# Level products on quarters of the array's columns, with a weight rounding and a bank eviction moved earlier in each head

## The reference

```
o_inter = einsum('bhtk,bhkv->bhtv', qb * exp(cum), state)
rel     = cum[t] - cum[s]                      # cum = cumsum(log_f)
decay   = exp(where(tri, rel, -inf))
scores  = einsum('bhtk,bhsk,bhtsk->bhts', qb, kb, decay)
o       = o_inter + einsum('bhts,bhsv->bhtv', scores, vb)
state   = state * exp(last) + einsum('bhsk,bhsv->bhkv', kb * exp(last - cum), vb)
```

## Time and profile before

| | |
|---|---|
| median of three runs | 2038.23 us |
| the profiled execution, its own time | 2038.05 us |
| its span in the trace | 2036.3 us |
| PE busy | 2027.9 us, 100% (rounded) of the span |
| DVE, ACT, POOL busy | 974.2, 785.8, 855.4 us |
| granted clock of TensorE | 1.0 of full speed |

### The profile page before, as it was taken

One profiled execution on the slowest core, in us unless ns is written; L12 is line 12 of the kernel. 1 busy time (PEld: TensorE's weight loads), 2 busy tenths in 40 slices (PEclk: granted clock), 3 DMA queues, 4 the chain that ended last, 5 costly groups with the idle time before them and its releaser, 6 DMA issues.

```text
span 2036.3 us, 24472 instructions
## 1 busy us (share of the span) xinstructions
PE 2027.9 (100%) x9822; PEld 1659.3 (81%) x9822; DVE 974.2 (48%) x1486; ACT 785.8 (39%) x1128; POOL 855.4 (42%) x357
## 2 busy tenths in 40 slices
PE   9999999999999999999999999999999999999999
PEld 7888888888888888888888888888877788888887
DVE  4588878634321313434463242454366646324242
ACT  6455656534222224522432222246266643222222
POOL 4334333544444444444444444453422234444444
PEclk9999999999999999999999999999999999999999
DMA  5222222342323232222323223232311122322323
GB/s 178 83 83 74 75 92 73 125 146 86 108 94 97 93 102 95 94 96 90 104 94 104 93 93 104 93 114 93 94 62 55 56 77 93 104 93 95 103 93 114
DMA packets 55265, 194.31 MB, mean 95 GB/s; under 512 B 6128, under 2 KB 6640, under 8 KB 55152
## 3 DMA queue, kind: packets, MB, share of 16 engines
q1 hardware_dynamic: 55152, 192.75, 29.4%
HBM read 190.62 MB, written 2.10 MB: 95 GB/s over the span
## 4 chain that ended last, share of the span: by engine, by line
PE 97%; DVE 1%; ACT 0%; DMA 0%; SPq 0%; issue 0%; DVEq 0%
PE ps L1356 30%; PE ps L1358 29%; PE ps L1357 29%; PE ps L1682 1%; PE ps L1715 1%; PE ps L1706 1%; PE ps L1644 1%; PE ps L1643 1%; PE ps L1642 1%; PE ps L1492 1%; PE ps L1364 0%; PE ps L1394 0%; PE ps L1514 0%; DMA w_raw<-in_panels 0%; PE ps L1516 0%; PE ps L1501 0%
## 5 line engine op out<-in xcount | busy, mean ns | idle before, releaser
L352 POOL TENSOR_TENSOR w_lo<-w_raw,w_hi 128x1024 fp32r<-128x1024 f32 x353 | 855.2, 2426 | 1169.0 <-ACT w_hi L371 1149.6
L1356 PE MATMUL ps<-a_hi,w_hi 128*128 128x512 f32 x1472 | 581.0, 395 | 2.2 <-DVE arena L783 1.9
L1358 PE MATMUL ps<-a_hi,w_lo 128*128 128x512 f32 x1472 | 573.5, 390 | 0.0
L1357 PE MATMUL ps<-a_lo,w_hi 128*128 128x512 f32 x1472 | 573.3, 389 | 0.0
L371 ACT CAST w_hi<-w_raw 128x1024 fp32r<-128x1024 f32 x353 | 366.2, 1042 | 323.7 <-PE ps L1358 290.9
L1356 PE MATMUL ps<-b_hi,w_hi 128*128 128x512 f32 x1176 | 458.5, 390 | 0.3 <-DVE x L817 0.2
L1358 PE MATMUL ps<-b_hi,w_lo 128*128 128x512 f32 x1176 | 457.6, 389 | 0.0
L1357 PE MATMUL ps<-b_lo,w_hi 128*128 128x512 f32 x1176 | 457.5, 389 | 0.0
L783 DVE TENSOR_TENSOR arena<-ps,inv_rms 128x512 f32<-128x512 f32 x200 | 138.0, 691 | 427.8 <-PE ps L1358 404.3
L1356 PEld LDWEIGHTS ps<-a_hi,w_hi 128*128 128x128 f32 x1472 | 276.4, 188 | 63.3 <-issue 5.5
L1357 PEld LDWEIGHTS ps<-a_lo,w_hi 128*128 128x128 f32 x1472 | 276.5, 188 | 58.0 <-issue 2.2
(11 more groups left out here) (201 smaller groups left out, 1599.3 us busy)
## 6 DMA issues: line engine op xcount, KB each, us to landing
w_raw<-in_panels SPq DMA_DIRECT2D x353, 512.0 KB, 3.5
x<-in_xT SPq DMA_DIRECT2D x16, 256.0 KB, 2.8
outT<-x SPq DMA_DIRECT2D x7, 256.0 KB, 2.0
consts<-in_const SPq DMA_DIRECT2D x1, 528.5 KB, 8.3
arena<-in_rows SPq DMA_DIRECT2D x1, 256.0 KB, 4.4
arena<-in_ws SPq DMA_DIRECT2D x1, 256.0 KB, 4.8
outT<-x SPq DMA_DIRECT2D x2, 128.0 KB, 1.8
consts<-in_late SPq DMA_DIRECT2D x1, 168.0 KB, 2.6
```

What stands on the lines that cost most here:

```text
L352: nc.gpsimd.tensor_tensor(w_lo[:, p % RING, :], w_raw[:, p % RING, :], w_hi[:, p % RING, :].bitcast(F), ALU.subtract).then_inc(w_low, 1)
L1356: nc.tensor.matmul(o, wh, hi[:, kt, :], start=(kt == 0), stop=False)
L1357: nc.tensor.matmul(o, wh, lo[:, kt, :], start=False, stop=False)
L1358: ins = nc.tensor.matmul(o, wl, hi[:, kt, :], start=False, stop=(kt == tiles - 1))
```

## The change

Three edits, all of them in the recurrent heads.

1. Levels from 1 up are multiplied in four runs of 32 keys in place of two of 64. Run s fills output partitions 32s to 32s+31, with 32 queries passed through it. Level 0 keeps two runs of 64. `later_of` picks 32 queries for each run.
2. ACT: in heads that have one behind them (1 to 7), panel p+6 is rounded before L496, and the square of the last output also goes ahead of it.
3. DVE: the bank of panel p+4 is emptied before all decays in head 0, and between decays 4 and 5 in the others.

```diff
 # ACT, head(h, a)
+                if a is not None:
+                    high(p + 6)
+                    square_output(a)
                 act.wait_ge(spans_done, h * 3 + 2)
                 nc.scalar.activation(qk[:, 2:6, :], qk[:, 2:6, :], ACT.Exp).then_inc(decays_done, 1)
-                if a is not None:
-                    square_output(a)
-                else:
-
+                if a is None:
                     high(p + 6)
...
                 if a is not None:
-                    high(p + 6)
                     root(R_HEAD + a, ps[:, 2, :], 1.0 / P, o_inv[:, :])
 # DVE, head(h, a)
+                if a is None:
+                    fill_out(p + 4)
                 dve.wait_ge(q_done, h + 1)
                 dve.wait_ge(decays_done, h * 4 + 2)
                 decay_queries([1, 2, 3, 4])
+                if a is not None:
+                    fill_out(p + 4)
                 dve.wait_ge(decays_done, h * 4 + 3)
                 decay_queries([5, 6, 7])
...
                 v.tensor_tensor(qk[:, 1, :], qk[:, 1, :], q[:, :], ALU.mult).then_inc(queries_decayed, 1)
-                fill_out(p + 4)
 # PE
             def later_of(cols, n, s):
                 if n == 0:
                     return cols[:, s * HEAD_DIM:(s + 1) * HEAD_DIM]
-                quarters = cols.rearrange("p (c n) -> p c n", c=4)
-                return quarters[:, 1:3, :] if s else quarters[:, 0:4:3, :]
+                if n == 1:
+                    first = (0, 3, 1, 2)[s] * HEAD_DIM // 2
+                    return cols[:, first:first + HEAD_DIM // 2]
+                eighths = cols.rearrange("p (c n) -> p c n", c=8)
+                return eighths[:, 3:5, :] if s == 3 else eighths[:, s:8 - s:7 - 2 * s, :]
...
-                        to = at * 2 * P + j * P
-                        for s in range(2):
-                            keys = qk[:, 2 + n, j * P + s * HEAD_DIM:j * P + (s + 1) * HEAD_DIM]
+                        to, size = at * 2 * P + j * P, HEAD_DIM if n == 0 else HEAD_DIM // 2
+                        for s in range(P // size):
+                            keys = qk[:, 2 + n, j * P + s * size:j * P + (s + 1) * size]
                             later = later_of(qk[:, 2 + n, SEQ // 2 + j * P:SEQ // 2 + (j + 1) * P], n, s)
-                            ins = nc.tensor.matmul(later_of(ps[half_of(s), 4 + gr % 2, to:to + P], n, s), keys, later,
-                                                   start=True, stop=True)
+                            ins = nc.tensor.matmul(later_of(ps[s * size:(s + 1) * size, 4 + gr % 2, to:to + P], n, s),
+                                                   keys, later, start=True, stop=True)
```

## The result

The changed kernel takes 2044.41 us (median of 8 runs, 2043.6 to 2044.81) against 2038.08 us (8 runs of the kernel before): ratio 1.0027, 95% interval 1.0019 to 1.0036. It is slower by 6.3 us. I forecast 2032.8, faster; what came is rival C, told there as 2045.4. The profiled execution took 2043.95 us with a span of 2042.2.

A forecast was written before the change was run, and what follows sets the result against it. PE, busy all through the span, was taken to bound the kernel. Gains of 1.9 us for head 0, 3.4 for edit 1 and 0 for edit 2 sum to 5.3: 2038.05 becomes 2032.8 us, range 2031.0 to 2046.0.

The forecast's parts named there:

- rival C: POOL takes its turn inside DVE's run, delaying panel p+3's eviction; PE waits 1.8 us in heads 1-7, 2045.4; chance 0.22.
- Edit 3, head 0: PE's whole 1.87 us wait for DVE's L783 before head 1 goes: 1.9 us less.
- Edit 1, the step: Level products from 1 up on PE: four 32-column records side by side, 0.032 us a step, 0.62 less a head.
- the change of width: New change between level 0 (64) and level 1 (32) on PE: costs 0.14 us a head, leaving net 0.48.
- B: Quarters run two at a time: 2.3 us more in all, less 1.9 for head 0: 2038.5, no change; chance 0.21.
- D: Each small record keeps 0.028 us: 12.0 us more in all, less 1.9 for head 0: 2048.2; chance 0.10.
- Edit 1, head 7: PE already waits 0.25 us for an eviction before product p+4, so head 7's 0.48 us gain is waited away.
- Edit 2, the failed step: POOL's part of p+6 waits out DVE's run to 167.03, ends at 169.4; evictions stay in time, price nothing.
- Edit 2, what it was for: Panel p+6 has 0.3 us slack before PE; without this edit half of the 0.48 us gain would be waited away.
- Edit 3, the middle heads: Outside head 0 it moves an eviction that PE did not wait for; costs DVE nothing.

The follow-up runs named there:

- e1: The kernel before with only the level products changed, to quarters of the columns; 2037.64 us, ratio 0.9994.
- e5: The changed kernel with the square of the last output ahead of the rounding of panel p+6; 2043.86 us, ratio 1.0026.
- e8: The changed kernel with the square ahead of the rounding of panel p+6 and computed four times over; 2042.53 us, ratio 1.0017.
- e11: The changed kernel with the square first, repeated over 512 columns and then over 64 x h columns in head h; 2043.96 us (one run).
- e12: e8 once more, with nothing changed; 2042.78 us (one run).
- e2: The kernel before with only ACT's order changed: panel p+6 rounded and last output squared before the exp of levels 0 to 3; 2047.4 us, ratio 1.0044.
- e7: The changed kernel with DVE's eviction of panel p+3 ahead of the spans of levels 4 to 6 in every head; 2033.51 us, ratio 0.9975.
- e3: The kernel before with only the emptying of panel p+4's bank moved: before the decays in head 0, between decays 4 and 5 elsewhere; 2037.38 us, ratio 0.9995.
- e6: The changed kernel with the rounding of p+6 right behind the exp of levels 0 to 3, square still ahead of it; 2032.63 us, ratio 0.997.
- e9: The changed kernel with the moves of e6 and e7 together; 2033.12 us, ratio 0.9975.
- e10: e6 with the level products on halves again, as in the kernel before; 2035.45 us, ratio 0.9987.

## Why the prediction was wrong

- **Edit 3, head 0.** Right: 1.9 forecast, 2.03 measured in the stage, in all kernels that have it. The 1.87 counts from the end of the last record; from start to start it is 95.34 - 93.08 = 2.26, less the usual 0.23.
- **Edit 1, the step.** Right: 0.034 us for four records of 32 columns (0.032 forecast), 0.16 for the change of width (0.14), 0.41 a head in place of 0.48 when nothing else is late. Rivals B and D are refuted by the 0.009 us between records and the step of 0.034, and with D what I worked out from the Trainium skill, "TensorEngine Tiling (Array Packing)", section "Instruction Overhead": its 60 cycles, 25 ns by my estimate, are no floor for each matmul when they go to different columns of the array, for here a matmul (two records) came every 18 ns on average.
- **Edit 1, head 7.** The gain was to be waited away, by a start 0.7 us behind the last record of p+3. It came at 365.14, with 364.22 for the last: 0.92. In e1 that head gained nothing, by this wait (0.94 there).
- **Edit 2, the failed step.** "I take it that POOL waits to 167.03 and runs to 169.4." It did not wait: it ran right behind the stalled L941, DVE's next L944 took 2.61 us, and the eviction of p+3, which I took to stay in time, came 2.2 us late. The price of this was worked out under rival C, 1.8 us in each of seven heads (its own numbers, 169.9 less 168.2, give 1.7), 12.6 in all, and 2045.4; PE's stage of a middle head grew by 1.25 us, that is 1.66 of wait less the 0.41 of edit 1. I had weighed one record that waited through a run of spans (83.91) and the 3.60 us of head 2 against one that didn't wait (87.87), and gave C 0.22. The record of head 2, and the three like it in heads 1, 3 and 4, met other operations (L870 or L875, L1053), so the evidence in spans was one against one. In the spans of heads 1 to 7, in five kernels (changed, e5, e8, e11, e12), 33 of 35 were let in, and in e2 and e7 14 of 14. By the Trainium skill, "SBUF — State Buffer", section "SBUF: two separate sides", whichever of the two starts first holds the ports for its whole instruction. Read as no longer than that, the rule would have said so, and I set it aside for a single row; the requests that were held do not fit it.
- **Edit 2, what it was for.** Right in kind: without it half of edit 1's gain was to be lost by a slack of 0.3 us. In fact nearly all was lost in heads 2 to 4 (e1: 0.02 to 0.05 of 0.41).
- **Edit 3, the middle heads.** "It costs DVE nothing": true of DVE, but POOL's turn hung on the operation that moved. e3 lost 1.75 us in heads 1 to 5, read as an effect of that from its POOL records of 4.18 us; in the changed kernel edit 2 hides it, since p+6 is ready long before.

So of the 6.3 us: edit 3 gives about 2.0, edit 1 about 0.4 in each of heads 1 to 6 and once behind them, and the collision takes 1.6 to 1.7 in each of seven heads: 7 x 1.66 - 2.0 - 2.9 = 6.7, near enough to the 6.5 by which the stages grew.

## What to carry to other kernels

When a transfer or a rounding is moved earlier, look at what its last engine shares with the engine whose result is due next. In these traces a DVE operation on two SBUF inputs could lose a whole POOL operation's time, 2.61 us in place of 0.41; put the eviction that the busiest engine needs ahead of that place, or start the POOL operation behind it. With the same early rounding the kernel took 2044.4 or 2033.5 us (e7), by which side of the collision one eviction stood on.

Where another engine delivers only 0.3 us before PE needs it, a gain of PE beyond that can't be had, and here not even that much came. And an operation that does nothing for the critical engine can still be the one that lets another in.

## What was not expected of the hardware

Four streams of 32 columns ran side by side in float32, a record every 9 ns on average, in steps of 0.034 us. A POOL operation that meets a run of DVE's two-input operations is mostly let in at a boundary: in the spans of heads 1 to 7 47 of 49 times, over seven kernels. But in head 0 a rounding at the same kind of spans was held for 0.87 us in every kernel profiled, and in the decays of e6, e9 and e10 it was held in seven heads of seven each. What decides between the two was not found.

In e6 the stage behind the heads gave back what edit 1 brings there (28.61 against 28.20 in e1). The time went between the starts of panels 57 and 58, 3.19 us against 2.85, and it is the collision once more. DVE and PE of e6 there:

```profile
373.12 1.42 DVE L963 SCALAR_TENSOR_TENSOR arena<-arena 128x512 f32<-128x512 f32 x1
374.46 0.68 DVE L957 TENSOR_TENSOR arena<-arena,ps 128x512 f32<-128x512 f32 x1
```

```profile
375.28 0.47 PE L1356 MATMUL ps<-gm_hi,w_hi 128*128 128x512 f32 x1 [0.18 <-DVE arena L957]
```

and DVE of e1:

```profile
376.91 0.69 DVE L966 SCALAR_TENSOR_TENSOR arena<-arena 128x512 f32<-128x512 f32 x1
```

In e6 POOL works on panels 57 and 58 until 373.98, and DVE's operation, which began at 373.12, takes 1.42 us in place of 0.69; the eviction of panel 56 behind it is late, and PE waits for it. In e1 POOL was done at 376.80, just before DVE's operation. In e7 the same operation takes 2.20 us, PE waits 0.57, and the stage is 29.44. No run moved this collision away.
